# A hybrid decoder trunk on one core: the S5 recurrence taken in steps of two tokens, and the experts' row stores issued by GpSimd

## The chip, the cores and the metric

The kernel runs on one core of a Trainium2 chip. The metric is the device time of one execution in microseconds (us). The kernel before takes 1588.45 us, the median of three executions (1587.74 to 1588.94).

## What is computed

Two layers over 256 tokens of width 1024, all in float32. Each layer projects the tokens once (`h = x @ w_in[l]`, 2956 columns), splits the columns among three mixers (S5, an attention, a gated DeltaNet), joins their outputs with one output projection and a layer norm, and then runs a SwiGLU channel mixer: dense in layer 0, the best two of eight experts in layer 1. The change touches the S5 mixer. Cut to that:

```
def s5_mixer(u, ...):
    lam_bar = jnp.exp(lam * step)                      # 16 groups x 64 complex states
    b_bar = ((lam_bar - 1.0) / lam)[..., None] * b_mat
    bu = einsum('blgp,gnp->blgn', ug, b_bar)           # 256 tokens, 16 inputs a group
    states: s[t] = lam_bar * s[t-1] + bu[t]            # over the 256 tokens
    y = einsum('gpn,blgn->blgp', c_mat, states).real + d_skip * ug
    y = gelu(y);  return y * sigmoid(y @ glu_w + glu_b)

out = sum over experts e of combine[..., e] * swiglu(x, w_gate[e], w_up[e], w_down[e])
```

## The kernel before

The engines run hand-written instruction streams that meet at semaphores; nothing is scheduled by a planner, so the order within an engine is the order of the program. `ps` is the whole PSUM (8 banks of 512 float32 columns); `arena` is one large SBUF buffer out of which nearly all tiles are cut, so the trace calls most tiles `arena`.

**Mixer, front part.** TensorE transposes x (`transpose_x`, L1654), then projects: `features(bank, ...)` (L1664) makes two halves of 128 features by 256 tokens with eight products each, `tokens(...)` (L1671) makes 128 tokens by up to 396 features. Between these stand the S5 input product `s5_in(t)` (L1838, four state tiles for each t, one 32-row group of TensorE for each), the attention scores (L1861, L1862, six heads) and sums of squares for the DeltaNet (L1880). ScalarE evacuates the projections (`evac`, L777), takes the exponentials of the scores (L799) and the activations. VectorE does the S5 work in two halves: `s5_rotate` turns the input by a phase table (L1108, L1118, L1119), `s5_recur` runs eight scans of 256 tokens, one for each state tile of the half and each of the real and the imaginary part (L1128), `s5_turn` turns the states back (L1148 to L1153). Beside that it does the convolution taps (`convolve`, L1083 and L1085), moves the scores out of PSUM (L1275 to L1277) and prepares the DeltaNet's gates (L1137 to L1140, L1290 to L1304). In layer 0 VectorE first works out the S5 parameters (`s5_parameters`, L1007 to L1055) and the phase table (`phase_table`, L557 to L583, by doubling up to 256 tokens); `c_padded` (L1063 to L1071) makes the output matrix. The table of layer 1 is made by GpSimd during the dense channel mixer.

**Mixer, back part.** The DeltaNet's triangular inverse (L1905 to L2021) with S5's output product `s5_out(f)` (L1915, four 32-column groups of TensorE) between its steps, its recurrence over four chunks, and the output projection (L2105, L2109).

**Channel mixers.** Weights stream in as pieces of 1 MB (SyncE issues the DMAs), ScalarE rounds each piece to its high part (L682), VectorE takes the low part (L1185), and TensorE forms three products from them (L1693 inward, L1704 outward). After each of the first seven experts ScalarE copies the result to `ye` (L743), waits for the copy and issues a store to the DRAM table `y_rows` itself (L746). After the seventh, GpSimd gathers rows of `y_rows` (L655), and VectorE adds them to x during the last expert (L1236).

At the start GpSimd issues the loads of `params` (L595), and, once the first chunk of w_in is in, of the constants, `s5_b` and `glu_w` (L597 to L599); in layer 1 those of `s5_b` and `glu_w` when the dense mixer's last piece is used (L603, L604).

## Time and profile before

| | |
|---|---|
| median of 3 executions | 1588.45 us |
| the profiled execution | 1587.36 us, of which the span of its instructions 1585.6 us |
| TensorE busy | 1544.8 us (97%), granted clock 0.995 |
| VectorE busy | 1263.5 us (80%) |
| ScalarE busy | 934.9 us (59%) |
| GpSimd busy | 114.3 us (7%) |
| mixer of layer 0 | about 0 to 185 us of the span |
| dense channel mixer | about 185 to 422 us |
| mixer of layer 1 | about 422 to 603 us |
| experts and last norm | about 603 to 1586 us |

PE is TensorE, PEld its weight loads, DVE VectorE, ACT ScalarE, POOL GpSimd, SP SyncE. A float32 product shows as two matmul records; a record's duration holds the latency of the array, so the pace of a row of products is read from start to start. All times in rows are counted from the start of the span.

### The profile page before, as it was taken

Reading aid. Unit: us, or ns where it says so; the run is one execution under the profiler, and the core shown is the slowest. Engines: PE = TensorE matmul, PEld = TensorE weight load, DVE = VectorE, ACT = ScalarE, POOL = GpSimd, SP = SyncE. Lnnn points to the kernel's source line nnn. Section 1 sums busy time; section 2 is a strip of 40 time slices with the busy share of each in tenths; the row PEclk is TensorE's granted clock in tenths of the full one; section 3 lists DMA queues with packets and bytes.
Section 4 is the critical chain, followed back from the end, with each engine's and each line's share of the span. In section 5 each row is a group of like instructions: output and inputs, shape, how many; then the busy total and the mean of one; then the engine's idle time right before and its main releaser. Section 6 shows DMA issues by size and latency. Waiting matters only on the chain.

```text
span 1585.6 us, 23114 instructions
## 1 busy us (share of the span) xinstructions
PE 1544.8 (97%) x8892; PEld 1255.4 (79%) x8892; DVE 1263.5 (80%) x1211; ACT 934.9 (59%) x795; POOL 114.3 (7%) x138
## 2 busy tenths in 40 slices
PE   8998999999999899999999999999999999999996
PEld 6777687888787767888888888888888888888875
DVE  6996755444539786888888888888888888888897
ACT  1264153444206424777777777777777777777775
POOL 0012193000000401000000000000000000000101
PEclk9999999999999999999999999999999999999999
DMA  8412578775443035999999999999999999999994
GB/s 328 161 54 82 197 285 307 278 284 189 159 161 107 4 133 189 397 393 395 395 395 363 395 394 347 395 395 346 395 395 348 395 395 345 395 395 358 396 393 177
DMA packets 190453, 472.27 MB, mean 298 GB/s; under 512 B 7632, under 2 KB 11856, under 8 KB 189328
## 3 DMA queue, kind: packets, MB, share of 16 engines
q1 hardware_dynamic: 186352, 454.23, 77.2%
q0 software_dynamic: 3024, 13.42, 2.2%
q10 hardware_dynamic: 1008, 3.67, 0.6%
q8 instruction: 47, 0.77, 0.2%
q14 instruction: 22, 0.18, 0.0%
HBM read 463.43 MB, written 25.69 MB: 308 GB/s over the span
## 4 chain that ended last, share of the span: by engine, by line
PE 84%; DVE 10%; issue 2%; ACT 2%; DMA 1%; ACTq 0%; SPq 0%; DVEq 0%; POOLq 0%
PE ps L1693 45%; PE ps L1704 24%; PE ps L1664 4%; DVE arena L1085 2%; PE ps L1766 2%; DVE lo L1185 1%; PE ps L2109 1%; PE ps L2105 1%; PE ps L1671 1%; ACT hi L682 1%; DVE arena L1108 1%; DVE arena L1128 1%; PE ps L2005 1%; PE ps L1685 0%; DMA x<-in_x_in 0%
## 5 line engine op out<-in xcount | busy, mean ns | idle before, releaser
L1185 DVE TENSOR_TENSOR lo<-arena,hi 128x2048 fp32r<-128x2048 f32 x378 | 868.5, 2303 | 205.6 <-ACT hi L682 204.5
L682 ACT ACTIVATE hi<-arena 128x2048 fp32r<-128x2048 f32 x378 | 723.7, 1918 | 355.3 <-PE ps L1693 219.9
L1693 PE MATMUL ps<-hi,xg 128*128 128x512 f32 x1760 | 543.6, 390 | 0.6 <-DVE lo L1185 0.2
L1693 PEld LDWEIGHTS ps<-hi,xg 128*128 128x128 f32 x1760 | 329.0, 188 | 71.2 <-DVE lo L1185 3.7
L1693 PE MATMUL ps<-lo,xg 128*128 128x512 f32 x880 | 342.4, 389 | 0.0
L1704 PE MATMUL ps<-hi,hTe 128*128 128x512 f32 x896 | 282.4, 396 | 0.0
L1693 PEld LDWEIGHTS ps<-lo,xg 128*128 128x128 f32 x880 | 165.2, 188 | 34.5
L1704 PEld LDWEIGHTS ps<-hi,hTe 128*128 128x128 f32 x896 | 164.1, 188 | 31.9
L1704 PE MATMUL ps<-lo,hTe 128*128 128x512 f32 x448 | 175.1, 391 | 0.0
L1693 PE MATMUL ps<-hi,xs 128*128 128x512 f32 x512 | 158.5, 391 | 3.2 <-issue 2.1
L1664 PE MATMUL ps<-arena 128*128 128x256 f32 x544 | 120.4, 383 | 2.0 <-DVE arena L1180 1.0
L1664 PEld LDWEIGHTS ps<-arena 128*128 128x128 f32 x544 | 104.0, 192 | 18.8 <-issue 3.4
L1693 PEld LDWEIGHTS ps<-hi,xs 128*128 128x128 f32 x512 | 95.5, 188 | 23.4 <-issue 4.0
L1693 PE MATMUL ps<-lo,xs 128*128 128x512 f32 x256 | 99.7, 389 | 0.0
L1704 PEld LDWEIGHTS ps<-lo,hTe 128*128 128x128 f32 x448 | 84.1, 188 | 18.8
L1704 PE MATMUL ps<-hi,hTd 128*128 128x512 f32 x224 | 69.5, 391 | 0.0
L655 POOL DMA_INDIRECT arena<-y_rows,row_of x4 | 7.7, 1926 | 849.3 <-DMA y_rows<-arena 848.4
L777 ACT ACTIVATE arena<-ps 128x512 f32<-128x512 f32 (+2 forms) x26 | 14.1, 543 | 92.7 <-PE ps L1664 76.4
L1693 PEld LDWEIGHTS ps<-lo,xs 128*128 128x128 f32 x256 | 48.1, 188 | 10.1
L1704 PEld LDWEIGHTS ps<-hi,hTd 128*128 128x128 f32 x224 | 41.6, 188 | 8.3
L1671 PE MATMUL ps<-arena 128*128 128x396 f32 (+1 forms) x128 | 43.0, 493 | 0.8 <-ACT arena L921 0.8
L1704 PE MATMUL ps<-lo,hTd 128*128 128x512 f32 x112 | 43.6, 389 | 0.0
(383 smaller groups left out, 1319.6 us busy)
## 6 DMA issues: line engine op xcount, KB each, us to landing
arena<-in_mg SPq DMA_DIRECT2D x112, 1024.0 KB, 7.6
arena<-in_mu SPq DMA_DIRECT2D x112, 1024.0 KB, 8.2
arena<-in_md SPq DMA_DIRECT2D x112, 1024.0 KB, 7.3
arena<-in_w_in SPq DMA_DIRECT2D x7, 2048.0 KB, 11.3
arena<-in_wg SPq DMA_DIRECT2D x14, 1024.0 KB, 5.8
arena<-in_wu SPq DMA_DIRECT2D x14, 1024.0 KB, 5.4
arena<-in_wd SPq DMA_DIRECT2D x14, 1024.0 KB, 5.3
xg_rows<-in_zeros SPq DMA_DIRECT2D x17, 512.0 KB, 7.2
```

Source lines behind the costliest of these rows:

```text
L682: af(hi[r % PARTS][:, :], raw[r % RAWS], ACT.Copy).then_inc(hi_ready, 1)
L1085: ins = stt(qkv[:, c, :], cin[:, c, w:w + T], cw[:, c, w:w + 1], qkv[:, c, :], ALU.mult, ALU.add)
L1108: ins = tt(turned_by, bu, table[:, two, :].unsqueeze(2).to_broadcast([P, 2, 2, T]), ALU.mult)
L1128: step(v_.tensor_tensor_scan(mt[2 * k + 1][:, jj * T:(jj + 1) * T], rad, mt[2 * k][:, jj * T:(jj + 1) * T], 0.0, ALU.mult, ALU.add))
L1185: tt(lo[r % PARTS][:, :], raw[r % RAWS], hi[r % PARTS][:, :].bitcast(F32), ALU.subtract)\
L1664: ins = mm(ps[:, bank, col:col + T], w[:, k, c0:c0 + P], xT[:, k, :], start=(k == 0), stop=(k == KT - 1))
L1671: ins = mm(ps[:, bank, 0:n], xT[:, k, b * P:(b + 1) * P], w[:, k, c0:c0 + n], start=(k == 0), stop=(k == KT - 1))
L1693: ins = mm(ps[:, (4 if w == "G" else 4 + nb) + b, :], tok[a][:, kk * nt + b * P:kk * nt + (b + 1) * P], tiles_of(part[r % PARTS], w)[:, k, ...
L1704: ins = mm(ps[:, 2 * b + c, :], hT[a][:, h0:h0 + P], tiles_of(part[r % PARTS], "D")[:, q, 512 * c:512 * (c + 1)], start=(j == 0 and p == 0 ...
L1766: ins = tr(ps[:, 6, q * P:(q + 1) * P], hh[:, q * P:(q + 1) * P], ident)
L2005: mm(ps[chunk_rows(c), bank, c0:c0 + CH], U[mine, i, :], A[mine, i, :], start=True, stop=True)
L2105: ins = mm(ps[:, (0, 1, 2, 5)[bank_at], :], mix_parts[k // 2][a][:, t0:t0 + P], wo_parts[part][:, 1024 * k + 512 * c:1024 * k + 512 * (c + ...
```

## The change

The recurrence is taken over pairs of tokens: the scans, the phase table and the rotations run over 128 steps in place of 256, for all eight state tiles. For that, lambda squared takes the place of lambda in `s5_parameters` (twelve more small instructions), and three small matrices are made on the chip in each layer. `s5_matrices` (VectorE, in place of `c_padded`) forms lambda B and two output matrices, C and C lambda. `stepped_matrices` (TensorE, new) turns lambda B by 16 products with the identity as moving operand (128 columns each) and forms C B by 16 products of 32 columns; ScalarE copies both out of PSUM (`b_step`, `d_mat`). It stands after `features(2)` in layer 0 and after `features(4)` in layer 1. `s5_in` is one block of 32 products of 128 columns in place of two blocks of 8 products of 256 columns. The even token of a pair gets its output from the state before the pair by C lambda, plus a direct product of C B with the input. `uT` is stored with even and odd tokens apart. The order on VectorE changes: both halves of S5 run before the first convolution, so that the second half no longer stands between the later ones.

`s5_b` grows from 256 to 768 KB a layer and is loaded as soon as the first half of the first w_in chunk is in; `params` loses 256 KB. The stores of the first seven experts' rows, and the wait for them, move from ScalarE's queue to GpSimd's.

```diff
...
+            pool.wait_ge(half_loaded, 16)
+            pool.dma_start(b_all, s5_b[0]).then_inc(b_loaded, 16)
             pool.wait_ge(slot_loaded[0], 16)
...
+            pool.wait_ge(y_stored, 16)
+            for e in range(NE - 1):
+                pool.wait_ge(ye_ready, 2 * (e + 1))
+                pool.dma_start(y_rows[e * P:(e + 1) * P, :], ye).then_inc(rows_stored, 16)
+            pool.wait_ge(rows_stored, ALL_ROWS)
...
+                    act.wait_ge(rows_stored, i * 16 + 64)
...
-                rows = y_rows[i * P:(i + 1) * P, :] if isinstance(i, int) else y_rows[bass.ds(i * P, P), :]
-                act.dma_start(rows, ye).then_inc(y_stored, 16)
+                if second:
+                    act.wait_ge(ye_ready, i * 2)
+                    rows = y_rows[i * P:(i + 1) * P, :] if isinstance(i, int) else y_rows[bass.ds(i * P, P), :]
+                    act.dma_start(rows, ye).then_inc(y_stored, 16)
...
+                def stepped_matrices():
+                    act.wait_ge(sb_psum, l + 1)
+                    af(b_step, ps[:, 7, :].rearrange("p (t r s) -> p t r s", t=2, r=2), ACT.Copy).then_inc(sb_evac, 1)
...
+                step(tt(rad, rad, rad, ALU.mult))
+                step(ts(lr, xr, 1.0, None, ALU.add))
+                step(tt(t1, pr, pr, ALU.mult))
+                step.then(tt(t2, pi, pi, ALU.mult))
+                step(stt(pi, pi, 2.0, pr, ALU.mult, ALU.mult))
+                step(tt(t0, fi, xi, ALU.mult))
+                step(tt(gr, fr, lr, ALU.mult))
+                step.then(tt(gi, fr, xi, ALU.mult))
+                step(tt(pr, t1, t2, ALU.subtract))
+                step(tt(gr, gr, t0, ALU.subtract))
+                step.then(tt(k_, fi, lr, ALU.mult))
...
+            def s5_matrices(l):
+                def per_state(k):
+                    return s5s[:, 16 * k + 8 * l:16 * k + 8 * l + 8].unsqueeze(2)
+                wide, one = [P, ST, 64], [P, ST, 32]
+                lam, f, g = (21, 23), (18, 19), (0, 1)
+                dve.wait_ge(b_loaded, 16 * (l + 1))
+                prod = [[halves[h][2 * i + k].rearrange("p (j r f) -> p j r f", j=ST, r=2) for k in range(2)]
+                        for h, i in ((0, 0), (0, 1), (1, 0))]
+                for p_, src, (re, im) in zip(prod, (b_state, c_state, c_state), (lam, f, g)):
+                    for k, by in enumerate((re, im)):
+                        ins = tt(p_[k].rearrange("p j r f -> p j (r f)"), src.rearrange("p j r f -> p j (r f)"),
+                                 per_state(by).to_broadcast(wide), ALU.mult)
+                        step(ins)
+                step.wait()
+                (b0, b1), *c01 = prod
+                step(tt(bl[:, :, 0, :], b0[:, :, 0, :], b1[:, :, 1, :], ALU.subtract))
+                step(tt(bl[:, :, 1, :], b0[:, :, 1, :], b1[:, :, 0, :], ALU.add))
+                for w, (c0, c1) in enumerate(c01):
+                    step(tt(c_mat[:, w, :, 0, :], c0[:, :, 0, :], c1[:, :, 1, :], ALU.subtract))
+                    ins = stt(c_mat[:, w, :, 1, :], c0[:, :, 1, :], -1.0, c1[:, :, 0, :], ALU.mult, ALU.subtract)
+                    if w == 0:
                         step(ins)
                 ins.then_inc(c_ready, 1)
...
+            def s5_rotate(l, a):
+                mt = halves[a]
+                dve.wait_ge(bu_psum, l + 1)
+                bank, four = (6, 0)[a], slice(4 * a, 4 * a + 4)
+                bu = ps[:, bank:bank + 2, :].rearrange("p b (j r t) -> p (b j) r t", j=2, r=2)
+                for k, table in enumerate((cos_t, sin_t)):
+                    ins = tt(turns[a][:, :, k, :, :].rearrange("p r j t -> p j r t"), bu,
+                             table[:, four, :].unsqueeze(2).to_broadcast([P, 4, 2, TT]), ALU.mult)
+                    if k:
+                        ins.then_inc(bu_used, 1)
+                    else:
+                        step(ins)
+                dve.wait_ge(bu_used, 2 * l + a + 1)
                 step.wait()
                 step(tt(mt[0], mt[0], mt[3], ALU.add))
                 step.then(tt(mt[2], mt[2], mt[1], ALU.subtract))
...
+            def s5_recur(l, a):
+                mt = halves[a]
+                for n in range(4):
+                    r0 = 16 * 20 + 8 * l + 4 * a + n
+                    rad = s5s[:, r0:r0 + 1].to_broadcast([P, TT])
                     for k in range(2):
-                        step(v_.tensor_tensor_scan(mt[2 * k + 1][:, jj * T:(jj + 1) * T], rad,
-                                                   mt[2 * k][:, jj * T:(jj + 1) * T], 0.0, ALU.mult, ALU.add))
+                        step(v_.tensor_tensor_scan(mt[2 * k + 1][:, n * TT:(n + 1) * TT], rad,
+                                                   mt[2 * k][:, n * TT:(n + 1) * TT], 0.0, ALU.mult, ALU.add))
...
+                s5_matrices(l)
+                if l == 0:
                     phase_table(v_, step, 0)
...
                 s5_rotate(l, 0)
+                s5_rotate(l, 1)
                 s5_recur(l, 0)
                 s5_turn(l, 0)
+                s5_recur(l, 1)
+                s5_turn(l, 1)
...
-                s5_rotate(l, 1)
+                dve.wait_ge(sc_exp, 2 * NH * (l + 1))
+                v_.reciprocal(rinv, rsum).then_inc(sc_norm, 1)
                 convolve(l, 4)
-                s5_recur(l, 1)
-                s5_turn(l, 1)
+                gates_in(l)
...
+                def stepped_matrices():
+                    pe.wait_ge(c_ready, l + 1)
+                    if l:
+                        pe.wait_ge(proj_evac, 14)
+                    for n in range(ST):
+                        jj, t = divmod(n, 2)
+                        own = slice(32 * jj, 32 * jj + 32)
+                        for r in range(2):
+                            mm(ps[own, 7, (2 * t + r) * P:(2 * t + r + 1) * P], bl[:, n, r, :], ident, start=True, stop=True)
+                    for n in range(ST):
+                        jj, t = divmod(n, 2)
+                        own = slice(32 * jj, 32 * jj + 32)
+                        for r in range(2):
+                            ins = mm(ps[own, 1, 32 * t:32 * t + 32], b_state[:, n, r, :], c_mat[:, 0, n, r, :],
+                                     start=(r == 0), stop=(r == 1))
+                    ins.then_inc(sb_psum, 1)
+                def s5_in():
+                    pe.wait_ge(proj_evac, 14 * l + 1)
+                    pe.wait_ge(sb_evac, 2 * (l + 1))
+                    for t in range(2):
+                        for r in range(2):
+                            for w_, stationary in enumerate((b_step, b_mat)):
+                                for jj, bank in enumerate((6, 7, 0, 1)):
+                                    rows = slice(32 * jj, 32 * jj + 32)
+                                    ins = mm(ps[:, bank, (2 * t + r) * TT:(2 * t + r + 1) * TT], stationary[rows, t, r, :],
+                                             uT[rows, t, w_, :], start=(w_ == 0), stop=(w_ == 1))
+                    ins.then_inc(bu_psum, 1)
+                if l:
+                    stepped_matrices()
                 features(5, 0, w[0], 2 * P)
                 features(5, T, w[0], 3 * P).then_inc(proj_psum, 1)
+                if l:
+                    s5_in()
...
                 features(2, T, w[1], P).then_inc(proj_psum, 1)
+                if l == 0:
+                    stepped_matrices()
                 features(3, 0, w[1], 2 * P)
                 features(3, T, w[1], 3 * P).then_inc(proj_psum, 1)
...
+                if l == 0:
+                    s5_in()
...
+                pe.wait_ge(bu_used, 2 * l + 2)
...
-                pe.wait_ge(proj_evac, 13 * l + 8)
-                pe.wait_ge(sc_evac, NH * l + 2)
-                s5_in(1)
...
+                    def out(q, w_, c0=0):
+                        return ps[32 * q:32 * q + 32, 4, f * T + w_ * TT + c0:f * T + (w_ + 1) * TT]
+                    for q in range(4):
+                        rows = slice(32 * q, 32 * q + 32)
+                        mm(out(q, 0), d_mat[rows, f, :], uT[rows, f, 0, :], start=True, stop=False)
+                    for w_ in range(2):
+                        for k, r in enumerate((0, 1, 0, 1)):
+                            for q in range(4):
+                                n = 2 * q + f
+                                state = halves[n // 4][k][:, (n % 4) * TT:(n % 4 + 1) * TT]
+                                ins = mm(out(q, w_, 1 - w_), c_mat[:, 1 - w_, n, r, :], state[:, 0:TT - 1 + w_],
+                                         start=(w_ == 1 and k == 0), stop=(k == 3))
                     return ins
...
```

## Rows read from the trace of the kernel before

**Rows 1.** The page's parts 1 and 4: busy time; the chain that ended last.
```profile
PE 1544.8 (97%) x8892; PEld 1255.4 (79%) x8892; DVE 1263.5 (80%) x1211; ACT 934.9 (59%) x795; POOL 114.3 (7%) x138
...
PE 84%; DVE 10%; issue 2%; ACT 2%; DMA 1%; ACTq 0%; SPq 0%; DVEq 0%; POOLq 0%
```

**Rows 2.** The chain in order of time (start us, us, what), layer 0.
```profile
1.65 7.00 DMA x<-in_x_in
...
67.89 0.29 DVE score_rows L1275
```

**Rows 3.** Stretches: length, busy time (instructions) by engine, clock, DMA share, GB/s.
```profile
11.67:106.00 94.33, 93.53 (x462) 72.95 (x462) 89.25 (x245) 30.63 (x72) 1.60 (x3) 1.00 0.53 195
...
620.00:1500.00 880.00, 877.12 (x3994) 723.52 (x3994) 772.82 (x436) 653.92 (x434) 12.06 (x9) 1.00 1.02 382
```

**Rows 4.** TensorE in order of time, layer 0: start, us, form, records, [idle before].
```profile
11.67 29.29 PE L1664 MATMUL ps<-arena 128*128 128x256 f32 x128 [1.00 <-DVE arena L1180]
40.89 1.15 PE L1838 MATMUL ps<-arena 32*128 32x256 f32 x16
...
66.29 0.50 PE L1861 MATMUL ps<-arena 64*128 64x128 f32 x4
...
69.32 1.15 PE L1838 MATMUL ps<-arena 32*128 32x256 f32 x16 [0.68 <-DVE score_rows L1277]
70.50 14.05 PE L1664 MATMUL ps<-arena 128*128 128x256 f32 x64
...
95.03 2.74 PE L1880 MATMUL ps<-arena,cst 128*128 128x512 f32 x6
...
103.64 0.96 PE L1893 MATMUL ps<-small,cst 128*128 128x12 f32 x8
104.67 1.54 PE L1905 MATMUL ps<-arena 64*64 64x128 f32 x48
106.14 1.93 PE L1915 MATMUL ps<-arena 128*32 128x256 f32 x32
```

**Rows 5.** TensorE in order of time: small products of later stretches.
```profile
145.53 0.87 PE L2127 MATMUL ps<-arena 128*64 128x128 f32 x6
146.23 0.82 PE L2132 MATMUL ps<-arena 128*64 128x128 f32 x6
...
603.48 3.64 PE L2198 MATMUL ps<-par,arena 128*128 128x8 f32 x32
```

**Rows 6.** VectorE in order of time, layer 0.
```profile
30.27 0.42 DVE L569 TENSOR_TENSOR arena<-arena,s5s 128x256 f32<-128x256 f32 x1
...
33.56 0.68 DVE L569 TENSOR_TENSOR arena<-arena,s5s 128x512 f32<-128x512 f32 x1
...
88.98 4.76 DVE L1128 TENSOR_TENSOR_SCAN arena<-s5s,arena 128x256 f32<-128x256 f32 x8
...
103.67 0.95 DVE L1304 TENSOR_TENSOR arena<-arena 128x768 f32<-128x768 f32 x1
```

**Rows 7.** TensorE in order of time, layer 1.
```profile
430.86 27.86 PE L1664 MATMUL ps<-arena 128*128 128x256 f32 x128 [0.90 <-ACT arena L921]
...
481.71 1.15 PE L1838 MATMUL ps<-arena 32*128 32x256 f32 x16 [0.47 <-DVE score_rows L1277]
```

**Rows 8.** VectorE in order of time, layer 1.
```profile
430.82 0.48 DVE L1063 MEMSET arena<- 128x512 f32 x1
...
459.87 4.62 DVE L1108 TENSOR_TENSOR arena<-ps,arena 128x1024 f32<-128x1024 f32 x4 [26.63 <-PE ps L1838]
```

**Rows 9.** DMA issues by line: transfer, queue, count, KB each, median us to landing.
```profile
cst<-in_consts POOLq DMA_DIRECT2D x1, 896.0 KB, 7.0
```

**Rows 10.** In order of time: GpSimd held up, its gather, its first use.
```profile
198.94 2.25 POOL L576 TENSOR_TENSOR s5s<-s5s 128x8 f32<-128x8 f32 x1
...
1480.22 2.38 POOL L655 DMA_INDIRECT arena<-y_rows,row_of  x1 [0.30 <-issue]
...
1507.20 1.28 DVE L1236 SCALAR_TENSOR_TENSOR x<-arena,rt,x 128x1024 f32<-128x1024 f32 x1
```

More of the change, by code:

```diff
@@ L42 @@
 FILLS = 2 * 17 - 1
+ALL_ROWS = 64 + 16 * (NE - 1)
 ALPHA = float((2 * L) ** 0.25)
@@ L132 @@
 A_PHASE = A_ZF + 9248
-ARENA = A_PHASE + 2 * ST * T
+ARENA = A_PHASE + 4096
+TT = T // 2
+BW = 3 * 512
+TILE_OF = [4 * (n % 2) + n // 2 for n in range(ST)]
 A_RAW = A_SLOTS
@@ L184, in build @@
         lnrow = score_rows[:, 0:2 * D].rearrange("p (g d) -> p g d", g=2)
-        phase = arena[:, A_PHASE:A_PHASE + 2 * ST * T]
+        phase = arena[:, A_PHASE:A_PHASE + 2 * ST * TT]
         s5s = sb("s5s", 24 * L * ST)
@@ L562, in phase_table @@
             tmp = score_rows[:, 0:2048] if l else zs(O_M, 2048)
-            while k < T:
+            while k < TT:
                 a = tmp[:, 0:ST * k].rearrange("p (j t) -> p j t", j=ST)
@@ L1054, in s5_parameters @@
                 dve.wait_ge(s5_step, 2)
                 step.then(ts(nA, nA, -1.0, None, ALU.mult))
-            def c_padded(l):
-                cc = par[:, PO["c"] + 256 * l:PO["c"] + 256 * (l + 1)].rearrange("p (j r f) -> p j r f", j=ST, r=2)
-                fr, fi = (s5s[:, 16 * k + 8 * l:16 * k + 8 * l + 8].unsqueeze(2).to_broadcast([P, ST, 16])
-                          for k in (18, 19))
-                t = [halves[0][0][:, 128 * k:128 * (k + 1)].rearrange("p (j f) -> p j f", j=ST) for k in range(4)]
-                step(v_.memset(c_mat, 0.0))
-                step(tt(t[0], cc[:, :, 0, :], fr, ALU.mult))
-                step(tt(t[1], cc[:, :, 1, :], fi, ALU.mult))
-                step(tt(t[2], cc[:, :, 1, :], fr, ALU.mult))
-                step.then(tt(t[3], cc[:, :, 0, :], fi, ALU.mult))
-                for half in range(2):
-                    rows, own = slice(64 * half, 64 * half + 64), slice(16 * half, 16 * half + 16)
-                    step(tt(c_mat[rows, :, 0, own], t[0][rows], t[1][rows], ALU.subtract))
-                    ins = stt(c_mat[rows, :, 1, own], t[2][rows], -1.0, t[3][rows], ALU.mult, ALU.subtract)
-                    if half == 0:
+            def s5_matrices(l):
[19 more added lines that the diff above has]
+                    if w == 0:
@@ L1097, in convolve @@
                         tap(l, c, w)
[L1099 to L1116 removed]
+            def s5_rotate(l, a):
[8 more added lines that the diff above has]
+                        ins.then_inc(bu_used, 1)
+                    else:
+                        step(ins)
+                dve.wait_ge(bu_used, 2 * l + a + 1)
                 step.wait()
@@ L1830, in _ @@
                 features(2, T, w[1], P).then_inc(proj_psum, 1)
+                if l == 0:
+                    stepped_matrices()
                 features(3, 0, w[1], 2 * P)
                 features(3, T, w[1], 3 * P).then_inc(proj_psum, 1)
-                def s5_in(t):
-                    for r in range(2):
-                        for jj, bank in enumerate(((6, 7, 0, 1), (6, 7, 2, 3))[t]):
-                            rows = slice(32 * jj, 32 * jj + 32)
-                            ins = mm(ps[:, bank, r * T:(r + 1) * T], b_mat[rows, t, r, :], uT[rows, t, :], start=True,
-                                     stop=True)
-                    ins.then_inc(bu_psum, 1)
-                pe.wait_ge(b_loaded, 16 * (l + 1))
-                pe.wait_ge(proj_evac, 14 * l + 1)
-                s5_in(0)
+                if l == 0:
+                    s5_in()
                 pe.wait_ge(proj_evac, 14 * l + 2)
@@ L1911, in s5_out @@
                 def s5_out(f):
-                    for k, r in enumerate((0, 1, 0, 1)):
-                        for q in range(4):
-                            ins = mm(ps[32 * q:32 * q + 32, 4, f * T:(f + 1) * T], c_mat[:, 4 * f + q, r, :],
-                                     halves[f][k][:, q * T:(q + 1) * T], start=(k == 0), stop=(k == 3))
+                    def out(q, w_, c0=0):
[10 more added lines that the diff above has]
+                                         start=(w_ == 1 and k == 0), stop=(k == 3))
                     return ins
@@ L2267 @@
             j, half = divmod(g, 2)
-            c_lay[64 * half:64 * half + 64, :, j, r, :] = cc[:, g].transpose(2, 0, 1)
+            n, rows_, own = TILE_OF.index(j), slice(64 * half, 64 * half + 64), slice(16 * half, 16 * half + 16)
+            c_lay[:, rows_, n, r, own] = cc[:, g].transpose(0, 2, 1)
+            s_lay[:, rows_, n, r, own] = bb[:, g]
             f0 = 16 * (g % 8)
@@ L2283 @@
     arr["params"] = par
-    arr["s5_b"] = b_lay.reshape(L, P, 4 * P)
+    arr["s5_b"] = np.concatenate([a.reshape(L, P, 512) for a in (b_lay, s_lay, c_lay)], axis=2)
     arr["glu_w"] = np.asarray(s5_glu_w).reshape(L, 2, P, S5W).transpose(0, 2, 1, 3).reshape(L, P, 512)
```

122 lines of the change are left out of this document (50 added, 72 removed).

## The prediction

> **What bounds the kernel now.** I read the page first: TensorE is busy 97% of the span and carries 84% of the chain that ended last [rows 1]. A share over the whole span says nothing about one stage, so I cut the span into stretches. In layer 0 from 11.67 to 106 us TensorE is busy 93.53 of 94.33 us and VectorE 89.25; both look like the bound [rows 3]. The chain of waits names VectorE from 67.89 us on [rows 2]. The order of time settles it. TensorE's row has one gap in that stretch, 0.68 us before the second `s5_in` [rows 4]. Is the row itself stretched by hidden waits? 64 records of `features` take 14.05 us there, 0.220 us each, beside a full VectorE [rows 4]; in layer 1, 128 of them take 27.86 us, 0.218 each, while VectorE idles for 26.63 us [rows 7, 8]. The pace is the same, so TensorE is bound by its own work, and VectorE merely ends at the same moment: TensorE is free at 103.64 + 0.96 = 104.60 and VectorE at 103.67 + 0.95 = 104.62, and the next product starts at 104.67 [rows 4, 6]. The reader should see two full rows, of which only TensorE's cannot be shortened by taking work from the other. In the experts TensorE is busy 877.12 of 880 us [rows 3].
>
> **What VectorE saves.** The 16 scans of 256 steps become 16 of 128; the eight of one half took 4.76 us [rows 6], and the rotations, turns and the table's last doubling go or halve too. By the above, that is work beside a full TensorE. I cost it at nothing. After the last projection (T = 95.03 us) VectorE will have less to do before the gates, but TensorE's own row from T to 104.60 has no gap [rows 4], so at most 0.1 us a layer comes of it, and I take none.
>
> **What TensorE gets, per layer.** First, 16 products of 128 columns with the identity, 32 records. Four in a row go to the same 32-column group. The nearest row is L2127: products of 128 columns on a 64-column group, also one after another in one group, 6 records in 0.70 us from start to start, 0.117 each, and half of a 256-column record is 0.109 [rows 5, 7]. At 0.11 that is 3.5 us. The other end is L1915, where four groups take turns: 32 records of 256 columns in 1.93 us, 0.060 each, so 0.030 for half the columns and 1.0 us in all [rows 4]. I take 3.5, since the order does not take turns. Second, 16 products of 32 columns, 32 records. L2198, 8 columns but 128 columns of weights, shows 3.64 / 32 = 0.114 a record, so at most 3.6 us [rows 5]; the lower end is again 0.030, 1.0 us. With a quarter of both the weights and the moving columns I take 0.05, nearer to the low end: 1.6 us. Sum 5.1 us (2.0 to 7.3). All of it stands in the gap-free part of TensorE's row.
>
> A rule of the Trainium skill bears on the same place. "TensorEngine Tiling (Array Packing)", section Key Properties, says that different tiles can load weights and multiply in parallel. By it the products at the three changes of group would overlap, and the first block would be about 0.65 us shorter. The rows show such overlap only where neighbours always differ in group (L1915), and I leave the term alone.
>
> `s5_in`: two blocks of 1.15 us become one with 64 records of half the columns. If the pace halves, nothing changes; if it does not fall under the 0.060 of L1915, 64 records take 3.8 us, 1.6 more [rows 4]. I take 0 (-0.2 to +1.6). `s5_out`: per half, 64 state records at half of 0.060 are again 1.93 us, and eight records of the direct product add a little: +0.25 each, 0.5 a layer. At 0.045 a record it would be 72 x 0.045 = 3.2 us, 2.6 more a layer [rows 4].
>
> The wait at the scores: TensorE starts them at 66.29 and goes on with `features(0)` at 70.50, 4.21 us with 1.18 of `s5_in` among them, so 3.03 us without it [rows 4]. VectorE took the first head at 67.89 and released TensorE after the second at 69.32, at most 0.7 us a head [rows 2, 4]. In the new order TensorE waits for the fourth head. VectorE, now idle when the scores come, starts about 0.5 us after the first and needs 4 x 0.6 = 2.4 us: 2.9 to 3.0 us. So this stays as it is (-0.7 to +0.7).
>
> **What is hidden, and under what.** `s5_matrices` is six multiplications of 512 columns (0.68 us) and six of 256 (0.42 us): at most 6.6 us [rows 6]. In layer 1 it can start where `c_padded` started, 430.82 us, and ends by 437.4; TensorE comes to `stepped_matrices` after a quarter of its 27.86 us, at 437.8 [rows 7, 8]. The cover is thin: what is late shows one for one, at most 2 us if `s5_b` (768 KB) lands late; 896 KB took 7.0 us in a full queue [rows 9]. In layer 0 TensorE arrives after three quarters of 29.29 us, at 33.6 us [rows 4]; VectorE was already deep in the phase table at 30.27 us [rows 6], the twelve extra parameter steps and 6.6 us fit before, and the shorter table gives the time back. ScalarE's two copies run beside `features`.
>
> The start: `params` is 256 KB smaller, and it shares the queues with x, which lands 7.00 us after its issue and opens TensorE's row [rows 2]. At the 382 GB/s of the experts [rows 3] that is at most 0.7 us; I take -0.4.
>
> The stores: ScalarE loses the wait and the issue, but it is not the bound. GpSimd sometimes stands still beside VectorE: an operation of only 8 columns took 2.25 us [rows 10], about as long as 2048 columns would take VectorE at four times 0.68 less the overlaps. Five issues, each 2 us late, make 10 us. The last gather was issued at 1480.22 + 2.38 = 1482.6 us and is first used at 1507.20 [rows 10]; with 7.0 us of landing 17 us are left. So 0. The Trainium skill, "SBUF — State Buffer", section "SBUF: two separate sides", states that a VectorE operation in a two-port mode keeps GpSimd from writing its DMA descriptors; the 2.25 us agree, and the sum is the same by it.
>
> **The sum.** Per layer 5.1 + 0 + 0.5 + 0 = 5.6; two layers 11.2; start -0.4: +10.8 us. The profiled span 1585.6 becomes 1596.4. The median of the runs stands 1588.45 - 1585.6 = 2.85 us above that span: 1599.2 us.
>
> **The rivals.** (1) The small products overlap across column groups after all. For it: L1915's 0.060. Against: L2127. Then 2.0 - 0.2 - 0.7 + 0.1 = +1.2 a layer, and -0.7 at the start: +1.7, 1590.2 us. (2) Small records have a floor of pace, and `s5_in` and `s5_out` pay for being cut in twice as many. Half of the upper bounds: (7.3 + 5.1) / 2 + 0.8 + 1.5 = 8.5 a layer, +17, 1605 us. A late `s5_b` in layer 1 adds to the same side. (3) Faster: VectorE is the true bound between T and 104.67 us, because the two turns of S5 that stand between the gates (two multiplications of 1024 columns, 2.3 us at a little under twice 0.68 each) delay TensorE unseen, and the small products overlap as in (1). Then 1.2 - 2.3 = -1.1 a layer, with the start -2.9: 1585.5 us. It decides once TensorE's new work is below about 2.3 us a layer. Against it is the gap-free row [rows 4].
>
> **How the numbers follow.** Forecast 0.68, rival (1) 0.13, rival (2) 0.14, rival (3) 0.05. What a measurement of this kernel can tell from no change is about 0.2%, 3.2 us. The forecast and (2) lie above it; of (1) I give two thirds to no change and the rest to slower. That makes 0.05 faster, 0.09 the same, 0.86 slower. The range, 1590 to 1606 us, takes in the low ends of the unknown costs and most of (2).
>
> **What would show it.** Right: in both layers a row of 64 new small records of some 5 us in TensorE's order of time, T about 5 us later against the start of its projections, no gap before `stepped_matrices`, VectorE idle before the scores and again before the gates, experts unchanged within 1 us. Wrong, if the new records take 2 us or less, if the kk products start less than 4 us later in layer 0, if TensorE waits for `c_ready` in layer 1, or if the stretch of the experts changes its length.

## The result, and the profile after

The changed kernel takes 1590.03 us, the median of 20 executions (1588.13 to 1593.01), beside 1587.85 us for 20 of the kernel before: a ratio of 1.0015, 95% interval 1.0009 to 1.0022. It is slower by 2.2 us, where 10.8 us were forecast. Its profiled execution has a span of 1588.1 us. These are the page's busy times and chain:

```profile
PE 1548.3 (97%) x9244; PEld 1264.1 (80%) x9244; DVE 1231.5 (78%) x1210; ACT 936.4 (59%) x799; POOL 99.2 (6%) x134
...
PE 91%; DVE 5%; DMA 2%; issue 1%; ACT 1%; SPq 0%; DVEq 0%; ACTq 0%; POOLq 0%
```

Beside [rows 1]: VectorE lost 32 us of work and half of its part of the chain, TensorE gained 3.5 us. So the new work was small, and it went to the engine that sets the time. TensorE in order of time, layer 0, beside [rows 4] (start us, us, line, form, records; L1973 are the kk products, the first of the DeltaNet's inverse, L1905 in the kernel before):

```profile
35.10 2.13 PE L1879 MATMUL ps<-cst,arena 128*32 128x128 f32 x29
36.97 0.28 PE L1884 MATMUL ps<-arena 128*32 128x32 f32 x3
...
37.80 7.17 PE L1707 MATMUL ps<-arena 128*128 128x256 f32 x32
44.90 2.07 PE L1897 MATMUL ps<-arena 32*128 32x128 f32 x64
...
71.23 0.50 PE L1933 MATMUL ps<-arena 64*128 64x128 f32 x4
...
74.88 14.05 PE L1707 MATMUL ps<-arena 128*128 128x256 f32 x64 [1.31 <-DVE score_rows L1319]
...
108.90 1.54 PE L1973 MATMUL ps<-arena 64*64 64x128 f32 x48
110.37 0.42 PE L1986 MATMUL ps<-arena 32*32 32x128 f32 x8
```

`stepped_matrices` runs from 35.10 to 37.80: 2.70 us for 64 records, where I had 5.1. `s5_in` takes 44.90 to 46.90, 2.00 us for all four state tiles, where two blocks of 1.15 stood. The wait at the scores has grown from 0.68 to 1.31 us.

I cut each layer at the same marks in every profile taken. Apart from the stretches at half clock (below), the rows of layer 1, and those of layer 0 from `features(0)` on, repeat to a few hundredths of a microsecond, so effects far below the spread of the medians can be read. From start to start, in us:

| stretch | layer 1 before | layer 1 after | difference |
|---|---|---|---|
| start of the projections to the scores | 48.04 | 51.85 | +3.81 |
| scores to `features(0)` | 3.99 | 3.65 | -0.34 |
| `features(0)` to the kk products | 34.17 | 34.03 | -0.14 |
| kk products to the attention | 18.75 | 18.82 | +0.07 |

That is +3.40 in layer 1. In layer 0 the first row is not that steady: 54.58 to 56.06 us in ten profiles of the kernel before and its variants (mean 55.43), 59.07 to 59.85 in the three profiles that have the changed kernel's own work there (mean 59.36). That is +3.9, and I take layer 1's +3.81 for it. The second row is 4.21 in the first profile of the kernel before alone, and 3.64 or 3.65 in its nine others and in the changed kernel, so nothing. Layer 0 counts +3.74. Together 7.1 us. Three more differences stand outside these marks. The start: in ten profiles of before and its variants the projections begin at 11.30 to 12.56 us, mean 11.76; in eight of the changed kernel and its variants at 10.83 to 11.57, mean 11.20: -0.56. The dense stage: -1.2 (235.8 us against 236.8 to 237.2). The experts: -2.8. The half-clock stretches are left out. The sum is 7.1 - 0.6 - 1.2 - 2.8 = +2.5 us, and 2.2 were measured. The last two were not in my sum at all; the experiments look for their causes.

### The profile page after: what moved, and what is told of

Same layout as the page of the kernel before. It is cut to its first block, busy times and chain, and to the rows that moved or that the text cites. A ratio compares the mean times of both kernels' runs of the same rounds, so it can differ in the third digit from the quotient of the medians.

```text
span 1588.1 us, 23781 instructions
## 1 busy us (share of the span) xinstructions
PE 1548.3 (97%) x9244; PEld 1264.1 (80%) x9244; DVE 1231.5 (78%) x1210; ACT 936.4 (59%) x799; POOL 99.2 (6%) x134
## 4 chain that ended last, share of the span: by engine, by line
PE 91%; DVE 5%; DMA 2%; issue 1%; ACT 1%; SPq 0%; DVEq 0%; ACTq 0%; POOLq 0%
PE ps L1736 46%; PE ps L1747 23%; PE ps L1707 8%; PE ps L1714 3%; PE ps L1809 2%; PE ps L2186 1%; PE ps L2182 1%; DMA arena<-in_md 1%; DVE lo L1225 1%; DMA arena<-in_w_in 1%; PE ps L2082 0%; PE ps L1992 0%; PE ps L1728 0%; DVE arena L1133 0%; PE ps L2073 0%
## 5 line engine op out<-in xcount | busy, mean ns | idle before, releaser
L666 POOL DMA_DIRECT2D y_rows<-arena x7 | 3.8, 544 | 836.2 <-ACT arena L761 836.2
```

The lines of the kernel that those rows point to most:

```text
L666: pool.dma_start(y_rows[e * P:(e + 1) * P, :], ye).then_inc(rows_stored, 16)
```

## The experiments

All ratios are to runs of the kernel before on the same chip. First, the kernel before again:

> The kernel before, unchanged. It shows what of the differences between the two first profiles belongs to one execution. Theory: the two stretches of 3.41 us at half TensorE clock in the attention of both layers of before (123.78 and 536.79 us) follow from the 2.4 to 3.4 us that TensorE waits just before them, and come again at the same places; the stall of 1.1 us at 243 us in the dense stage is of that execution alone and is gone or elsewhere. Rival: the half-clock stretches fall at random places too, and a price cannot be put on their absence in the changed kernel. Ratio 1.000 against itself, within 0.0006.

Median 1587.47 us, ratio 1.0000 (0.9992 to 1.0009). Both halves of my expectation were wrong. Of the two stretches at half clock only the one in layer 1 came (535.49 us). The stall came again, at the same product and 1.11 us long: it belongs to the kernel.

### The stores

```
-                act.wait_ge(ye_ready, i * 2 + (0 if second else 2))
...
-                act.dma_start(rows, ye).then_inc(y_stored, 16)
...
+            for e in range(NE - 1):
+                pool.wait_ge(ye_ready, 2 * (e + 1))
+                pool.dma_start(y_rows[e * P:(e + 1) * P, :], ye).then_inc(x_scattered, 16)
```

> The kernel before with one part of the change alone: GpSimd issues the rows' stores of experts 0 to 6. Theory (the stores are worth 0.4 us an expert, because ScalarE no longer waits for its own copy and issues a DMA before the next high part): seven times 0.4, -2.4 to -2.8 us, ratio 0.9983 to 0.9985, the stretch of an expert 0.4 us shorter, and the wait of VectorE's first low part of an expert (1.74 us after ScalarE) down to 0.1. Rival (the step of the prediction: stores cost nothing, and the 0.4 us an expert came from some other place of the changed kernel): ratio 1.0000, within 0.0004.

1584.96 us against 1587.86: ratio 0.9982 (0.9973 to 0.9991), -2.9 us. And the other way round, the changed kernel with the old stores:

> The changed kernel with that one part undone: ScalarE issues all rows' stores again, so what is left is the S5 part alone. Theory: 2.4 to 2.8 us above the changed kernel, so 1.0030 to 1.0033 of the kernel before. Rival (stores cost nothing): as the changed kernel, 1.0015 of before.

1592.42 us, ratio 1.0036 (1.0023 to 1.0049): 4.6 us above before, 2.4 above the changed kernel. All engines in order of time at the end of an expert, kernel before:

```profile
751.29 1.06 ACT L743 ACTIVATE arena<-ps 128x512 f32<-128x512 f32 x2
...
752.54 0.40 ACTq L746 DMA_DIRECT2D y_rows<-arena  x1
...
753.50 3.72 ACT L682 ACTIVATE hi<-arena 128x2048 fp32r<-128x2048 f32 x2 [1.15 <-issue]
...
755.45 4.49 DVE L1185 TENSOR_TENSOR lo<-arena,hi 128x2048 fp32r<-128x2048 f32 x2 [1.74 <-ACT hi L682]
...
757.80 0.73 PE L1693 MATMUL ps<-hi,xg 128*128 128x512 f32 x2 [0.21 <-DVE lo L1185]
```

The same place with the stores on GpSimd:

```profile
750.27 1.06 ACT L751 ACTIVATE arena<-ps 128x512 f32<-128x512 f32 x2
...
751.22 1.92 ACT L687 ACTIVATE hi<-arena 128x2048 fp32r<-128x2048 f32 x1
751.94 0.59 POOL L656 DMA_DIRECT2D y_rows<-arena  x1 [127.43 <-ACT arena L751]
...
753.17 2.29 DVE L1194 TENSOR_TENSOR lo<-arena,hi 128x2048 fp32r<-128x2048 f32 x1 [0.48 <-ACT hi L687]
```

The reader should follow one delay through three engines. ScalarE starts the next high part 2.21 us after its first copy in before, 0.95 us after it without the store. VectorE's low part is late by as much, and at 757.80 the delay reaches TensorE: 0.21 us before the product (0.09 or 0.10 in the later experts). Most of it shows as no idle time at all, because TensorE's records overlap each other. The distance of this place from one expert to the next shows it whole: 118.99 us in the kernel before, 118.60 with the stores on GpSimd, 0.4 us an expert and 2.8 us over seven. Which of the two, the wait for the copy or the issue? Here the wait is put back:

```
+                act.wait_ge(ye_ready, i * 2 + (0 if second else 2))
                 if second:
-                    act.wait_ge(ye_ready, i * 2)
...
```

> The kernel before with the stores of experts 0 to 6 issued by GpSimd, as in the run before_gpsimd_stores, but with ScalarE's wait for its own last copy put back in front of its next high part; only the issue of the DMA is then gone from ScalarE. Theory W (the wait for the copy and the issue delay the high part by about 1.2 and 1.0 us; the slack of the low parts swallows the first): the stretch of an expert stays as short as without the wait, ratio 0.998. Rival (the wait alone already makes the low part late): 0.2 to 0.4 us an expert come back, ratio 0.999 to 1.000.

1585.27 us, ratio 0.9987 (0.9978 to 0.9996), and in the experts' rows no step against the run without the wait (118.60 us from expert to expert in both). The wait alone is swallowed; wait and issue together are not. The issue alone was not tried.

### The stepped matrices

```
-                    for n in range(ST):
-                        jj, t = divmod(n, 2)
+                    for k in range(16):
+                        jj, t, r = k % 4, k // 8, k // 4 % 2
+                        n = 2 * jj + t
...
```

> The changed kernel with the 32 products of the stepped matrices in another order: the four 32-column groups take turns instead of four products in a row on one group. The same instructions. Theory A (the 2.7 us a layer, 0.066 us a record where I had 0.11, come from overlap between groups, and only the group changes overlap now): the first block falls from 2.0 us to the 1.0 us of 0.030 a record, some 1.0 us a layer, ratio 1.0002 of before with everything else as in the changed kernel. Theory B (a record of 128 columns of weights x 32 simply costs 0.066 whatever its neighbour's group, since its weights are a quarter): no change, 1.0015, first block 2.0 us a layer as before.

TensorE in order of time, with the groups taking turns:

```profile
34.20 1.08 PE L1879 MATMUL ps<-cst,arena 128*32 128x128 f32 x32
35.10 0.48 PE L1885 MATMUL ps<-arena 128*32 128x32 f32 x32
35.51 7.17 PE L1707 MATMUL ps<-arena 128*128 128x256 f32 x32
```

From start to start 0.90 us for the first block and 0.41 for the second: 1.31 a layer instead of 2.70, the same in layer 1. The median, 1589.41 us, ratio 1.0006 (0.9997 to 1.0014), shows less than the 2.8 us of the rows. More half-clock time goes with that: nine of its twelve executions have a granted clock of 0.994, of the changed kernel's twenty only six. Why, no run shows. Now the other end:

```
-                            mm(ps[own, 7, (2 * t + r) * P:(2 * t + r + 1) * P], bl[:, n, r, :], ident, start=True, stop=True)
+                            mm(ps[0:32, 7, (2 * t + r) * P:(2 * t + r + 1) * P], bl[:, n, r, :], ident, start=True, stop=True)
```

> The changed kernel with all 16 products of the first block of the stepped matrices written to one 32-column group (three quarters of b_step are then not computed, and the output is of no use; the same 64 instructions). It asks where 0.066 us a record comes from. Theory A (a record costs 0.109 us behind one of its own group, and a group of four products begins while the four before it still run): nothing is left to overlap, 32 records take 32 x 0.109 = 3.5 us instead of 1.97, +1.5 us a layer in TensorE's row and +3 us in the time against the changed kernel. Theory B (small records of this kind simply cost 0.066 us): no change.

```profile
33.37 3.68 PE L1879 MATMUL ps<-cst,arena 128*32 128x128 f32 x32
36.88 0.88 PE L1884 MATMUL ps<-arena 128*32 128x32 f32 x32
```

3.52 us from start to start, 0.110 a record: what I had forecast for the block in its real order. 1594.45 us, ratio 1.0043 (1.0028 to 1.0059). So 0.11 was right for a neighbour of the same group. In the real order the records of a group still follow each other at 0.109 us, but the first record of the next group starts 0.47 us after that of the group before it, while that one needs 0.87 for its eight: half of each group lies beside the next. Changing groups is enough for that; the groups need not take turns. Theory B has fallen in both directions.

### What VectorE's savings are worth

> The kernel before with VectorE's 16 scans a layer over the first 128 of the 256 tokens alone (the states of the other tokens are left out). It gives VectorE back some 4.5 us a layer in the stretch between the last projection and the gates, and nothing else changes. Theory (the prediction's: TensorE's own full row sets the start of the kk products, VectorE is only level with it): at most 0.1 us a layer, ratio 1.0000 within 0.0004, the kk products of layer 0 start at the same distance from T (9.64 us). Rival 3 of the prediction (VectorE bounds that stretch unseen): 1 to 2.3 us a layer faster, ratio 0.9972 to 0.9987.

```
-                    rad = s5s[:, r0:r0 + 1].to_broadcast([P, T])
+                    rad = s5s[:, r0:r0 + 1].to_broadcast([P, P])
...
```

1586.44 us, ratio 0.9994 (0.9985 to 1.0003). `features(0)` to the kk products takes 34.03 us in both layers, as in the changed kernel, not 34.17: 0.14 us. In layer 1 the scores to `features(0)` fall from 3.99 to 3.65. So 0.6 us in all, and TensorE's row was what bounded the stretch. My third rival wanted 2.3 us a layer.

### The wait at the scores

> The changed kernel with the stepped matrices' products taking turns over the groups, and with the wait at the scores cut in two: the third head's scores free the bank of features(0), the fourth head's that of features(1), where the changed kernel waits for the fourth ahead of both. Theory (that wait is VectorE's pace of 0.6 to 0.7 us a head, exposed one for one): from the scores' start to features(0) 3.0 instead of 3.65 us in each layer, 1.2 us in all below after_turns, ratio 1.000 of before, or 0.999 where fewer stretches at half clock fall into the run. Rival (what follows is bound by something else late by the same 0.6 us): the kk products start where they did.

```
-                pe.wait_ge(sc_evac, NH * l + 4)
+                pe.wait_ge(sc_evac, NH * l + 3)
                 features(0, 0, w[4], 0)
                 features(0, T, w[4], P).then_inc(proj_psum, 1)
+                pe.wait_ge(sc_evac, NH * l + 4)
```

Scores to `features(0)` 3.06 us in both layers instead of 3.65, and all that follows keeps its distances. 1588.15 us, ratio 0.9999 (0.9990 to 1.0008). The fourth head costs 0.59 us a layer, one for one.

### The stall in the dense stage

TensorE stands still for 1.11 us before 243.16 us, and the profile names nothing that it waits for. The stall is there, 0.80 or 1.11 us long, in nine of the ten profiles of the kernel before and its variants (the tenth is the last run of this section), and in none of the eight of the changed kernel and its variants. My first guess was the place of the instruction in TensorE's stream, so I put products ahead of it (88 in one kernel, 8 in the other):

```
+                for k in range(88):
+                    own = slice(32 * (k % 4), 32 * (k % 4) + 32)
+                    mm(ps[own, 2, 48:60], C("same")[:, own], g_i, start=True, stop=True)
```

> The kernel before with 88 more products a layer (176 records, as many as the changed kernel has more than before), of 32 x 12 columns in turns over the four groups, ahead of the gates' sums; nothing reads them. Theory (the stall of 1.1 us on no visible cause at 243 us in the dense stage belongs to the place of the instruction in TensorE's stream): the stall is gone from there, as in the changed kernel. Rival (it belongs to something else, of the state of another engine or a queue, which the changed kernel has different): it stays at the same product, 1.1 us. The products themselves take 1 to 3 us a layer.

> The same with 8 more products a layer (16 records). Theory of the instruction's place: a shift this small moves the stall by at most a few products, or not at all. Rival as above: it stays at the same product.

Each was run once. In both the stall stayed at the same product, 1.11 and 0.80 us: the guess fell. (The 88 products themselves cost 3.1 and 4.0 us a layer, more than expected.) The order of time of the other engines shows another candidate, kernel before:

```profile
226.89 2.29 DVE L1185 TENSOR_TENSOR lo<-arena,hi 128x2048 fp32r<-128x2048 f32 x1 [3.15 <-ACT hi L682]
232.33 3.22 DVE L1185 TENSOR_TENSOR lo<-arena,hi 128x2048 fp32r<-128x2048 f32 x1 [0.79 <-ACT hi L682]
237.77 4.15 DVE L1185 TENSOR_TENSOR lo<-arena,hi 128x2048 fp32r<-128x2048 f32 x1 [2.22 <-ACT hi L682]
...
237.38 2.39 POOL L571 TENSOR_TENSOR arena<-score_rows 128x1024 f32<-128x1024 f32 x1
239.85 3.83 POOL L573 TENSOR_TENSOR score_rows<-arena,s5s 128x1024 f32<-128x1024 f32 x1
...
241.85 1.21 DVE L1209 TENSOR_TENSOR hTd<-ps,hTd 128x1024 fp32r<-128x1024 f32 x1
...
243.16 0.70 PE L1693 MATMUL ps<-hi,xs 128*128 128x512 f32 x2 [1.11 <-issue]
```

GpSimd makes the table of phases for layer 1 here, and its last doubling (1024 columns an operation) stands beside VectorE's low parts, which take 3.22 and 4.15 us instead of 2.29. The second of them starts at 237.77 us inside GpSimd's L571, which ends at 239.77, and ends 2.15 us after that, which is close to what it takes alone. The next of VectorE, L1209, is late with it. The program tells what TensorE waits for: `ht_lo`, the semaphore that L1209 raises. L1209 ends at 241.85 + 1.21 = 243.06 us, and the product starts 0.10 us later. The changed kernel's table ends one doubling earlier.

> The kernel before with GpSimd's table of phases for layer 1 ended at 128 steps, as in the changed kernel (the rest is set to zero at the start of the table, so layer 1's states of the later tokens are not computed). Theory (the operations of the last doubling hold up VectorE's low parts, and TensorE with them): VectorE's low parts between 225 and 246 us take 2.29 us each, the stall of TensorE at 243 us is gone, 1.1 to 1.3 us in the time, ratio 0.9992. Rival (the stall has yet another cause): it stays, ratio 1.0000.

```
-            k = 1
+            k, end = 1, T // 2 if l else T
...
-            while k < T:
+            while k < end:
```

1585.77 us, ratio 0.9986 (0.9977 to 0.9995). VectorE's low parts and TensorE, the same place:

```profile
231.67 2.29 DVE L1188 TENSOR_TENSOR lo<-arena,hi 128x2048 fp32r<-128x2048 f32 x1 [0.79 <-ACT hi L685]
237.11 2.29 DVE L1188 TENSOR_TENSOR lo<-arena,hi 128x2048 fp32r<-128x2048 f32 x1 [3.15 <-ACT hi L685]
239.32 1.22 DVE L1212 TENSOR_TENSOR hTd<-ps,hTd 128x1024 fp32r<-128x1024 f32 x1
...
241.23 0.62 PE L1696 MATMUL ps<-hi,xs 128*128 128x512 f32 x2
```

The stall is gone, and what TensorE waited for is ready at 239.32 + 1.22 = 240.54 us, 0.69 us before it is wanted. (Two low parts ahead of these took 2.97 and 3.08 us there, beside operations of 512 columns; they cost TensorE nothing.) In the rows the dense stage is 1.0 to 1.4 us shorter; the median is 2.7 us lower, with an interval from 0.8 to 3.7. That GpSimd's operations and VectorE's held each other up is what the two durations show. The Trainium skill, "SBUF — State Buffer", section "SBUF: two separate sides", gives a rule for it: the two share a pair of ports as an exclusive lock, and a VectorE operation with two SBUF inputs and a GpSimd operation that reads SBUF block each other for a whole instruction. The trace agrees in both directions: [rows 10] has GpSimd held for 2.25 us, beside a low part of 2.37 us, and here VectorE is.

### The clock, and a version that beats both

In the half-clock stretches the granted clock of TensorE is 0.5, 1.2 of 2.4 GHz, for 3.41 us. A view of stretches, kernel before (length, busy time by engine, clock, DMA share, GB/s):

```profile
120.60:123.78 3.18, 0.75 (x20) 0.69 (x22) 3.06 (x5) 0.22 (x1) 1.19 (x1) 1.00 0.00 0
123.78:127.19 3.41, 3.41 (x34) 3.41 (x33) 1.24 (x3) 0.16 (x1) 0.00 (x0) 0.50 0.00 0
```

TensorE was busy 0.75 of 3.18 us before it fell: it waits 2.44 us there for VectorE, which has four taps of the convolution ahead of the update that TensorE needs. The attention's 36 records then take 4.05 us to the next product (123.42 to 127.47), and 2.38 us at full clock in the changed kernel's profile (127.72 to 130.10): 1.7 us. The 14 profiles of kernels with the old place of the attention have such a stretch in 15 of their 28 attentions, and 12 of the 14 have one in the router stage, behind the router's 32 records of 8 columns (1.5 us). Much of the spread of the executions goes with it: of the changed kernel's 20 executions the six with a granted clock of 0.994 took 1591.5 to 1593.0 us, the other 14 took 1588.1 to 1590.4. A second series of it:

> The changed kernel, unchanged, on the chip of the two runs below. Theory: 1.0015 of before within 0.0008. Rows: from the start of the projections to the scores 51.85 us in layer 1 (48.04 in before), scores to features(0) 3.65, and so on to within 0.1 us, whatever the clock does elsewhere; the half-clock stretches may fall on other places than the router stage.

1591.31 us, ratio 1.0015 (1.0006 to 1.0025), three half-clock stretches in its profile, and the rows as before: 51.86, 3.64.

The attention needs nothing that TensorE waits for there, so it can fill the wait:

```
                     products_xy(v, 1)
+                    if v == 1:
+                        attention()
                     if v < 4:
                         product_a(v + 1, 0)
...
-                    if v == 1:
-                        attention()
```

> The kernel before with the stores of experts 0 to 6 issued by GpSimd, and with attention() moved ahead of product_a(2, 0), so that its 36 records run where TensorE waits 2.4 us a layer for VectorE. It asks two things: whether a kernel with the old S5 and the cheap half of the change beats both, and whether the half-clock stretch in the attention follows from that wait. Theory: 2.0 us a layer less (36 records at 0.055 us), less what VectorE then makes late: 1 to 2 us a layer; no half-clock stretch in the attention of either layer. With the stores 2.9 us below before already: ratio 0.996 to 0.997. Rival (VectorE's chain of the Y and X updates bounds the stretch, the wait only moves behind the attention): as before_gpsimd_stores, 0.9982.

1580.90 us, ratio 0.9955 (0.9941 to 0.9968). No half-clock stretch in the attention; from the start of `s5_out` to the channel mixer each layer takes 75.2 us where the run with the stores alone takes 76.9, so 1.7 us a layer. With the S5 part, its products in turns and the wait at the scores cut in two:

> The changed kernel with the products of the stepped matrices in turns, the wait at the scores cut in two, and attention() ahead of product_a(2, 0). In the changed kernel the new records of s5_out (+0.35 us a half) vanish in the wait of TensorE behind them: from the kk products to the attention 18.82 us where before has 18.75. Theory: with that wait filled they show, 0.5 to 0.7 us a layer; S5's part over before_attention_first is then 1.31 (stepped) - 0.25 (s5_in) - 0.6 (wait at the scores) - 0.1 (kk) + 0.6 = +1.0 us a layer, +2 us in all. Rival (VectorE, relieved by the shorter scans, lets the attention stretch run faster here): level with before_attention_first or below it.

1580.50 us, ratio 0.9950 (0.9937 to 0.9964). The 0.5 to 0.7 us a layer that this expectation gave `s5_out` did not come: from its start to the attention the old S5 takes 14.38 us and the new one 14.44 to 14.60. Since the two lay closer than their spread, both ran again:

> before_attention_first once more, beside the next run. Theory: 0.9955 of before within 0.001; no half-clock stretch in the attention of either layer (none in its first profile, where the kernel before had them in layer 0, layer 1 or both).

> after_attention_first once more, beside the run above. Theory (from the rows: layer 1 takes 1.4 us more than the old S5 between the start of the projections and the attention, layer 0 2.0 us, less 1.2 us for the stall that it lacks): 2 us above before_attention_again, 0.0013 of the time. Rival: level with it, within 0.0005, so that the row differences are given back somewhere.

1582.31 us, 0.9962 (0.9948 to 0.9975), and 1581.41 us, 0.9960 (0.9947 to 0.9974). In none of the four profiles is there a half-clock stretch in an attention, 0 of 8. Both kernels beat both of the given ones by more than 5 us. The S5 part, even improved, is level with the old one within what five executions tell: the rows' +2 us are not seen in the medians. In the profiles they are there: from the start of the projections to the attention the new S5 takes 1.4 and 1.5 us more in layer 1, 2.0 and 2.5 in layer 0, less 1.1 for the dense stage. What sets them off there is the router stage: both profiles of the old S5 have a half-clock stretch in it (3.41 and 6.83 us), neither of the new S5 has, and from the start of layer 1's channel mixer to TensorE's last record the old take 976.5 and 977.6 us, the new 974.5. Nothing shows that this belongs to the S5 part: with the attention in its old place all six profiles of the new S5 had that stretch.

## Why the prediction was wrong

The direction and the mechanism held: VectorE's savings were beside a full TensorE row, and TensorE's new work showed one for one. The size failed, by 8.6 us, at the steps below. Of the four signs of being wrong that I had named one came, the experts' stretch. The new records took 2.70 us, the kk products of layer 0 started 4.5 us later against the start of the projections in the first profiles (97.52 for 93.00), and TensorE never waited for `c_ready`; the first two kept clear of what I had called wrong by little.

**"What TensorE gets": the term that was mis-sized.** 5.1 us a layer forecast, 2.70 measured, 4.8 us in all. The failed sentence is "I take 3.5, since the order does not take turns". 0.11 us a record was right for one group (3.52 us when all went to one), but I applied it to a row that changes groups three times. The page of the Trainium skill that I weighed, "TensorEngine Tiling (Array Packing)", section Key Properties, spoke for overlap at exactly these changes. I priced it at 0.65 us and left it out, and it was worth more than twice that: 3.52 less 1.9 us. The second block, 16 products of 32 columns, took 0.8 us where I took 1.6; the lower end of 1.0 was still too high.

**`s5_in`, the scores and the joins: forecast 0, measured +0.8 to +1.1 a layer.** The records of `s5_in` did halve in price, 0.031 us. But one of its two blocks no longer lies behind the scores, where it filled time that VectorE needed anyway, and the fourth head adds 0.59 us to the wait. I had forecast 2.9 to 3.0 us from the scores to `features(0)`, and it took 3.65: VectorE took the first head 1.03 us after the scores' start (72.26 for 71.23), where I had taken 0.5. I had given ±0.7 for this wait and taken the middle.

**`s5_out`: forecast +0.5, measured +0.07 a layer.** The direct product takes 0.35 us a half (110.37 to 110.72), where I had 0.25. What I had wrong is that it shows one for one: the stretch behind it has slack. Counted from the start of the kk products, the second `s5_out` starts at 4.80 us in the kernel before and at 4.81 in the changed one, so the first 0.35 us is swallowed by then; a wait of 0.17 us for VectorE stood there before and is gone. The second 0.35 us is down to 0.07 at the third group of probabilities (13.25 and 13.32 us). The wait of 2.44 us stands behind that and is as long in both kernels. I read [rows 4] up to 106.14 us only and did not look for the gaps behind it.

**"What VectorE saves": nearly right for VectorE, wrong for GpSimd.** I took none and 0.14 us a layer came. But I wrote of "the table's last doubling" as VectorE's work alone. In layer 1 it is GpSimd's, beside the dense stage, and it cost TensorE 1.0 to 1.4 us. I had the row of such a collision [rows 10] and used it only for the stores' queue.

**The stores: forecast 0, measured -2.8.** "ScalarE loses the wait and the issue, but it is not the bound" is the failed sentence. It is not the bound by its busy time, but its high parts feed VectorE's low parts, and these feed TensorE with little to spare; of a delay of 1.3 us 0.4 passes through. That TensorE was busy for 877.12 of 880 us [rows 3] had seemed to leave no room. With the stores on GpSimd it is busy for 877.76 of the same 880, though each expert is 0.39 us shorter: a busy share made of overlapping records does not show such a delay, the distance between two experts does. My fear for GpSimd's queue was empty, too: the seven issues took 0.53 to 0.59 us each in the changed kernel. What I had set beside it from the Trainium skill, on descriptors, is shown by no run here; the 2.25 us of [rows 10] are an arithmetic operation of GpSimd beside a subtraction of VectorE.

**The start: forecast -0.4, measured -0.56.** Right in size; that the smaller `params` is the reason was not tried by itself. The hidden costs held: no wait for `c_ready` in the list of TensorE's waits, no late `s5_b`, and `s5_matrices` ended at 437.75 us in layer 1, 1.4 us before TensorE came to its products (439.18).

**The rivals.** Rival (1), small products overlapping across groups, was the right one: its 1590.2 us is the measured time within 0.2. But it got there with +1.2 us a layer and nothing from stores or table; the real sum is +3.6 a layer, less 4.0 us for stores and table. Its number is right by luck. Rivals (2) and (3) fell: no pace floor showed (0.013 us for the smallest records, in turns), and taking work from VectorE freed 0.14 us after T.

## What to carry to other kernels

A price per record holds only for the order in which it was read: look at which tile of the array each neighbour uses, and make small products change tiles. An engine that is busy 59% can still set the time if its one late operation starts a chain with less slack than the delay; follow the row of the consumer's consumer, from one round of the loop to the next and not by busy shares, before a moved DMA issue is costed at zero. And ask of each part of a change on which engines it runs: the same function ran on VectorE in one layer and on GpSimd in the other, and the second was the one that mattered.

## What the runs showed of the hardware that I had not expected

Records of 128x32 weights and 128 columns cost 0.110 us each when all go to one column group, about 0.06 with the group changing after every eighth, and 0.028 in turns; with 32 columns 0.025 in eights and 0.013 in turns. GpSimd beside VectorE's 2048-column subtraction stretched it from 2.29 to 4.15 us: 2.00 us until GpSimd's operation ended, 2.15 after. TensorE's granted clock fell to half for 3.41 us behind a wait of 2.44 us, in some executions and not in others, and cost 1.7 us there; with the wait filled it did not fall in any of eight attentions.
